# Residual sums bank by bank, a finer last gate and a reordered opening in a float32 encoder trunk

## What is computed

```python
h = x
for i in range(2):
    hn = rms_norm(h, norm_mix[i])
    if i == 0:
        h = h + concat(attention(hn @ w_in), conv(hn @ w_in)) @ w_out
        h = h + swiglu(rms_norm(h, norm_ffn[0]), wg, wu, wd)        # 1024 x 2816
    else:
        h = h + pool(hn) * pool_scale
        h = h + sum(gates[:, e] * swiglu(rms_norm(h, norm_ffn[1]), wg[e], wu[e], wd[e]) for e in range(8))
    gate = sigmoid(rms_norm(h, ple_norm[i]) @ ple_gate_w[i])        # 1024 x 1024
    h = h + gate * (p[i] @ ple_proj[i])                             # 256 x 1024
```

## Time and profile before

| | |
|---|---|
| median of 3 runs | 1361.47 us (1361.33 to 1363.37) |
| profiled execution | 1361.89 us |
| its span | 1360.1 us |
| TensorE busy | 1335.8 us, 98% |
| VectorE busy | 1156.1 us, 85% |
| ScalarE busy | 1008.5 us, 74% |
| granted TensorE clock | 0.999 |

### The profile page before, as it was taken

The page is one execution under the profiler, slowest core; times in us unless marked ns, Lnnn a source line. Parts: engine busy times, 40 slices in busy tenths (PEclk is TensorE's granted clock), DMA queues, the critical chain, the costliest instruction groups (busy, mean ns, idle before and its releaser), DMA issues.

```text
span 1360.1 us, 19059 instructions
## 1 busy us (share of the span) xinstructions
PE 1335.8 (98%) x6747; PEld 1126.5 (83%) x6747; DVE 1156.1 (85%) x1241; ACT 1008.5 (74%) x1188; POOL 46.9 (3%) x55
## 2 busy tenths in 40 slices
PE   7999999999999999999999999999999999999998
PEld 6868999988778888888888888888888888888886
DVE  6986555557799999999999999999999999999995
ACT  6866444446788887888888788888878888888874
POOL 1000000000050000000000000000000000000000
PEclk9999999999999999999999999999999999999999
DMA  9407853376799899999999999999999999999930
GB/s 350 163 1 272 301 186 124 125 250 235 110 379 397 309 394 395 374 360 396 394 339 394 395 374 359 396 395 339 394 395 374 359 396 394 394 393 398 400 122 33
DMA packets 178484, 427.03 MB, mean 314 GB/s; under 512 B 4096, under 2 KB 13568, under 8 KB 178432
## 3 DMA queue, kind: packets, MB, share of 16 engines
q1 hardware_dynamic: 173248, 412.10, 80.9%
q0 software_dynamic: 3168, 11.54, 3.3%
q10 hardware_dynamic: 2016, 2.72, 0.6%
HBM read 419.53 MB, written 6.82 MB: 313 GB/s over the span
## 4 chain that ended last, share of the span: by engine, by line
PE 91%; DVE 5%; ACT 2%; issue 1%; DMA 0%; SPq 0%; ACTq 0%; DVEq 0%
PE G L1366 18%; PE G L1368 18%; PE G L1367 18%; PE Y L1366 11%; PE Y L1368 11%; PE Y L1367 11%; PE G L1712 2%; DVE lo_ring L803 2%; DVE ring L863 1%; DMA ring<-in_w_in 0%; ACT xT_hi L504 0%; ACT tok L561 0%; DVE xT_lo L833 0%; ACT hi_ring L468 0%; DVE s_small L934 0%
## 5 line engine op out<-in xcount | busy, mean ns | idle before, releaser
L803 DVE TENSOR_TENSOR lo_ring<-ring,hi_ring 128x1024 fp32r<-128x1024 f32 x692 | 838.3, 1224 | 141.6 <-ACT hi_ring L468 100.1
L468 ACT ACTIVATE hi_ring<-ring 128x1024 fp32r<-128x1024 f32 x692 | 732.8, 1062 | 250.5 <-PE G L1368 149.0
L1366 PE MATMUL G<-hi_ring,xT_hi 128*128 128x512 f32 x896 | 353.9, 395 | 1.4 <-DVE lo_ring L803 0.8
L1368 PE MATMUL G<-lo_ring,xT_hi 128*128 128x512 f32 x896 | 349.5, 390 | 0.0
L1367 PE MATMUL G<-hi_ring,xT_lo 128*128 128x512 f32 x896 | 348.8, 389 | 0.0
L1366 PE MATMUL Y<-hi_ring,mT_hi 128*128 128x512 f32 x568 | 223.9, 394 | 0.0
L1368 PE MATMUL Y<-lo_ring,mT_hi 128*128 128x512 f32 x568 | 221.3, 390 | 0.0
L1367 PE MATMUL Y<-hi_ring,mT_lo 128*128 128x512 f32 x568 | 221.2, 389 | 0.0
L1366 PEld LDWEIGHTS G<-hi_ring,xT_hi 128*128 128x128 f32 x896 | 168.2, 188 | 36.0 <-DVE lo_ring L803 2.0
L1368 PEld LDWEIGHTS G<-lo_ring,xT_hi 128*128 128x128 f32 x896 | 168.3, 188 | 35.8
L1367 PEld LDWEIGHTS G<-hi_ring,xT_lo 128*128 128x128 f32 x896 | 168.4, 188 | 33.5
(11 more groups left out here) (251 smaller groups left out, 939.6 us busy)
## 6 DMA issues: line engine op xcount, KB each, us to landing
ring<-in_moe_wg SPq DMA_DIRECT2D x56, 2048.0 KB, 11.8
ring<-in_moe_wu SPq DMA_DIRECT2D x56, 2048.0 KB, 13.3
ring<-in_moe_wd SPq DMA_DIRECT2D x56, 2048.0 KB, 13.2
ring<-in_ffn_wg SPq DMA_DIRECT2D x5, 2048.0 KB, 11.5
ring<-in_ffn_wu SPq DMA_DIRECT2D x5, 2048.0 KB, 10.1
ring<-in_ffn_wd SPq DMA_DIRECT2D x5, 2048.0 KB, 7.9
ring<-in_ple_gate_w SPq DMA_DIRECT2D x4, 2048.0 KB, 7.8
ring<-in_w_out SPq DMA_DIRECT2D x2, 2048.0 KB, 13.4
```

What stands on the lines that cost most here:

```text
L468: act.activation(hi_ring[:, n % AHEAD, :], where, ACT.Copy).then_inc(hi_done, 1)
L803: dve.tensor_tensor(lo_ring[:, n % AHEAD, :], where, hi_ring[:, n % AHEAD, :].bitcast(F32), ALU.subtract).then_inc(lo_done, 1)
L1366: pe.matmul(dst, s_hi, m_hi, start=start, stop=False, skip_group_check=True)
L1368: return pe.matmul(dst, s_hi, m_lo, start=False, stop=stop, skip_group_check=True)
```

## The change

Five places are edited; what is computed stays the same.

1. Opening: TensorE transposes all eight blocks of token tile 0, then those of tile 1. ScalarE and VectorE make weight piece 0, four blocks, piece 1, four blocks.
2. Output projection: bank 2c + t takes the place of 2t + c, so that the left halves of both tiles are done first; the last two pieces go bank by bank. VectorE adds four times 512 columns; `half_ready` marks the left halves. The transposes of the left half wait for these, and those of the last two blocks for all. On ScalarE norm 1's copies go ahead of piece 25.
3. First gate: bank b's first product waits for the low copies of blocks 2b and 2b + 1.
4. Last expert and gate: the spread matmuls, the additions and the transposes go by column halves as in 2; the second projection piece is cut in two by token tiles, one behind each half of the transposes; the wait goes by banks as in 3; on VectorE the low copies go ahead of one low part; the last three pieces (two before) go bank by bank, behind one wait for their three low parts.
5. End: the last bank's sigmoid, product, addition and store are cut in two of 256 columns.

```diff
+HALVED = (1, 5)
+LAST_PARTS = ((0, 0, 512), (1, 0, 512), (2, 0, 512), (3, 0, 256), (3, 256, 512))
 # SP
-        for t, c0, c1, n in ((0, 0, D, 2), (1, 0, 512, 3), (1, 512, D, 4)):
+        for t, c0, c1, n in ((0, 0, D, 2), (1, 0, 512, 3), (1, 512, 768, 4), (1, 768, D, 5)):
 # ScalarE
         norm(0)
+        hi_upto(0)
+        act.wait_ge(vec_in, 16)
+        norm_hi(0, Y8, 0, KT // 2)
         hi_upto(1)
-        act.wait_ge(vec_in, 16)
-        norm_hi(0, Y8)
+        norm_hi(0, Y8, KT // 2, KT)
...
+        hi_upto(20 + AHEAD)
+        norm_hi(1, Y8)
         hi_upto(21 + AHEAD)
-        norm_hi(1, Y8)
         norm(1)
...
-        for b in range(2 * T):
+        for n, (b, c0, c1) in enumerate(LAST_PARTS):
...
-            act.activation(tok[:, b // 2, (b % 2) * 512:(b % 2 + 1) * 512], Y[:, b, :], ACT.Sigmoid,
+            act.activation(tok[:, b // 2, (b % 2) * 512 + c0:(b % 2) * 512 + c1], Y[:, b, c0:c1], ACT.Sigmoid,
 # VectorE
-        def add_rows(i, use, end):
+        def add_halves(i, use, end):
+            for c in range(2):
+                for t in range(T):
+                    b = 2 * c + t
+                    dve.wait_ge(bank_done, 3 * use + b + 1) if b < 3 else dve.wait_ge(pe_piece, end)
+                    dve.tensor_tensor(h[:, t, c * 512:(c + 1) * 512], h[:, t, c * 512:(c + 1) * 512], Y[:, b, :],
+                                      ALU.add).then_inc(h_ready if c else half_ready, 1)
...
+        lo_upto(0)
+        norm_lo(0, Y8, 0, KT // 2)
         lo_upto(1)
-        norm_lo(0, Y8)
+        norm_lo(0, Y8, KT // 2, KT)
...
-            for t in range(T):
-                dve.wait_ge(scat_mm, t + 1)
...
+            for c in range(2):
+                for t in range(T):
+                    part = h[:, t, c * 512:(c + 1) * 512]
+                    dve.wait_ge(scat_mm, 2 * c + t + 1)
...
+            norm_lo(5, Y8)
             last(XP + AHEAD)
-            norm_lo(5, Y8)
...
+        for n, (b, c0, c1) in enumerate(LAST_PARTS):
+            t, c = b // 2, slice((b % 2) * 512 + c0, (b % 2) * 512 + c1)
+            dve.wait_ge(sig_gate, 2 * T + n + 1)
+            link(dve.tensor_tensor(tok[:, t, c], tok[:, t, c], G[:, b, c0:c1], ALU.mult))
+            dve.tensor_tensor(h[:, t, c], h[:, t, c], tok[:, t, c], ALU.add).then_inc(gated, 1)
 # TensorE
+        def norm_half(i, bank, half):
...
+                for k in range(half * KT // 2, (half + 1) * KT // 2):
+                    if i in HALVED:
+                        if half == 0 and t == 0 and k % 2 == 0:
+                            pe.wait_ge(half_ready, T * HALVED.index(i) + k // 2 + 1)
+                        if half and t == 0 and k == KT - 2:
+                            pe.wait_ge(h_ready, T * (i + 1))
...
-        def rows(n, s_hi, s_lo, bank, first, last):
+        def rows(n, s_hi, s_lo, bank, first, last, freed=None):
...
+                    if freed is not None:
+                        pe.wait_ge(nlo_done, freed + 2 * (2 * t + c + 1))
...
+        def last_out_rows(n, e):
+            for u in range(2):
+                pe.wait_ge(lo_done, n + u + 1)
+            for c in range(2):
+                for t in range(T):
+                    for u in range(2):
+                        w_hi, w_lo = hi_ring[:, (n + u) % AHEAD, :], lo_ring[:, (n + u) % AHEAD, :]
+                        ins = three(Y[:, 2 * c + t, :], ...)
+                        if (c, t) == (1, T - 1):
+                            piece(n + u, ins)
+                    if (c, t) != (1, T - 1):
+                        ins.then_inc(bank_done, 1)
...
-        norm(0, Y8)
+        for t in range(T):
+            pe.wait_ge(tok_done, t + 1)
+            for k in range(KT):
+                ins = pe.transpose(Y8[:, k, t * P:(t + 1) * P], tok[:, t, k * P:(k + 1) * P], ident)
...
-            pe.wait_ge(nlo_done, KT * 3)
             for k in range(KT - 3):
-                rows(first + 2 + k, xT_hi[:, k, :], xT_lo[:, k, :], Y, k == 0, False)
+                rows(first + 2 + k, xT_hi[:, k, :], xT_lo[:, k, :], Y, k == 0, False, None if k else KT * 2)
...
-            norm(5, Y8)
-            last_rows_of(XP + 1, pT_hi[1][:, 1], pT_lo[1][:, 1], G, False, True)
-            pe.wait_ge(nlo_done, KT * 6)
+            for t in range(T):
+                norm_half(5, Y8, t)
+                last_rows_of(XP + 1, pT_hi[1][:, 1], pT_lo[1][:, 1], G, False, True, (t,))
...
+            for u in range(3):
+                pe.wait_ge(last_lo, XP + KT - 1 + u - AHEAD + 1)
+            for b in range(2 * T):
+                t, c = b // 2, slice((b % 2) * 512, (b % 2 + 1) * 512)
+                for u in range(3):
+                    q, k = XP + KT - 1 + u, KT - 3 + u
+                    ins = three(Y[:, b, :], ...)
```

More of the change, by code:

```diff
@@ L1044, in _ @@
         lo_upto(PB - 2)
-        gate(0)
+        gate()
         dve.wait_ge(gate_add, 2 * T)
@@ L1555, in _ @@
         ins.then_inc(mean_mm, 1)
-        rows(14, mT_hi[:, 0, :], mT_lo[:, 0, :], Y, True, False)
+        out_rows(14, 0, True)
         pe.wait_ge(sq_done, 1)
```

113 lines of the change are left out of this document (57 added, 56 removed).

## The result

The changed kernel takes 1356.01 us (median of 6 executions, 1355.69 to 1356.60) against 1361.42 (median of 6, 1361.10 to 1363.37): a ratio of 0.9955 on record, 95% interval 0.9944 to 0.9965 (the quotient of the two medians is 0.9960, inside it). The forecast was 1357.4, a fall of 4.1, in a range of 1356.0 to 1359.4; the fall is 5.4. The direction was right, the size was 1.4 us short, and the time lies on the lower edge of the range. The profiled execution takes 1355.81 us and its span is 1354.0; that of before took 1361.89, so the two profiles differ by 6.08.

A forecast was written before the change was run, and what follows sets the result against it. TensorE was taken to bound the kernel, with time to be had only where it stands still. 1.1 + 1.08 + 0 + 1.5 - 0.1 + 0.8 = 4.4 us off the profiled 1361.89 or median 1361.47 gave 1357.4, range 1356.0 to 1359.4.

The forecast's parts named there:

- Opening, 1.1: Before the first weight product: reordered transposes and copies start TensorE's products at 11.85, 1.1 us earlier (0 to 1.2).
- rival (a): Clock: the opening's first products run at half pace, losing 0.55 us, so 1357.9; chance 0.20.
- Output projection, 1.08: Residual after the output projection: banks by column half let copies start at 119.87, 1.08 us earlier (0.7 to 1.15).
- rival (b): Absorbed: ScalarE or VectorE takes up one of the two early gains, so 1358.5; chance 0.15.
- First gate, 0 (0 to 0.35): Dense half's first gate product: spread waits remove 0.34 us at 318.35, but TensorE waits longer at 333.82; no gain.
- Last expert, 1.5 (1.2 to 1.65): Residual before the last gate: idle falls from 1.8 to some 0.3 us, first gate product 1.5 earlier.
- The end, 0.8 (0.5 to 1.2): After the last matmul: last addition gains 0.6 us and the smaller store 0.2.
- passes stay: Sign in the seven expert passes: each stays at 119.04 us, or the prediction is wrong.
- no wait 36 matmuls from the end: Sign in the last gate: no wait before its last three pieces, for which 0.1 us (0 to 0.3) was charged.
- The wait at 333.82 longer: Sign behind the dense half's first gate: TensorE's wait for a low part there grows once the 0.34 at 318.35 goes.
- Rival (c): End edit fails: the three-piece wait costs 1.2 us, not 0.1, halves give 0.5, not 1.5; 1359.5; chance 0.10.
- rival (d): Slower: instructions come late at seven expert loop turns and the loop's end, 1.49 us each; 1369; chance 0.05.

The follow-up runs named there:

- e5: The changed kernel run and profiled again with no edit; 1357.05 us, ratio 0.9953 to the kernel before.
- e1: The kernel before run and profiled again with no edit; 1363.32 us median of 11, ratio 1.000.
- e13: The kernel before with nine transposes of a constant added ahead of the first real one; 1361.67 us, ratio 0.9995.
- e4: The kernel before with the six transfer issues (pooling scales and bands) moved from ScalarE's queue to GpSimd's; 1361.69 us, ratio 0.9996.
- e6: The changed kernel with the six transfer issues (pooling scales and bands) moved from ScalarE's queue to GpSimd's; 1356.13 us, ratio 0.9949.
- e2: The kernel before with only the first gate's waits by banks added; 1361.75 us median of 11, ratio 0.9994.
- e7: The changed kernel with the last bank of the final gate whole again and three stores for four; 1356.96 us, ratio 0.9956.
- e3: The changed kernel with the single wait for all low copies at the first gate put back; 1357.07 us median of 5, ratio 0.9956.
- e9: The changed kernel with the last gate's matmuls tile by tile over two pieces as before, last bank still split; 1357.56 us, ratio 0.9962.

## Why the prediction was right in direction and short in size

**Opening, 1.1:** right. The first product came at 11.91 (11.85 said), A moved by 1.04, and the shift at 50 was that at 13. The pitch behind it was 0.12 at once in the two first profiles, so rival (a) did not come in their times. Yet its mechanism is real: 4 to 7 products are slow in four of the other profiles with the new opening and 1 or 2 in two more (up to 0.8 us: the first 48 products take 5.83 in after and 6.61 in e5), and 22 in e1. What I had wrong is that I weighed it for the change alone. It burdens the kernel before more, by 2.1 us in half of its executions, and I had three times of that kernel before me, one of them 1363.37, and did not ask what set it apart.

**Output projection, 1.08:** right to the hundredth, with ScalarE's leeway of 0.28 where 0.3 was said. No rival (b).

**First gate, 0 (0 to 0.35):** this is the step that failed, 1.04 in the profiles and 0.9 to 1.06 in the medians. It failed twice. First, the claim that TensorE would only wait longer at 333.82, and so give the gain back, rested on one execution with a long transfer issue (1.47), which made ScalarE's chain late; e1 and e13 show the kernel before without that wait, and the chain has slack there. With the edit and short issues only 0.14 to 0.17 comes back at W2. Second, the bound of 0.35 took the idle time on the row as the price of the wait. The pair e4 and e6 prices it at 0.64: the idle is counted from the modelled end of the last matmul, 0.39 after its start, but without the wait the next one would start 0.23 after it, which adds 0.16, and the first matmul behind the wait is followed after 0.34, not 0.23, which adds 0.11. That makes 0.61. With W2's 0.20 of idle for 0.50, the two waits of the earlier trace rows were worth 1.15 and not 0.54. So of the 1.04 about half is the edit by itself (0.64 less the 0.16 at W2), which the bound of 0.35 also missed; the other half is the long issue's wait, which was in before's profile and not in after's. It goes in most executions and not in all (e2).

**Last expert, 1.5 (1.2 to 1.65):** the mechanism was right and the size off: 1.80 from C to D, with the 0.1 for three pieces already in it (0.05 to 0.1 measured), so about 1.9 for 1.5. Up to the gate's first product it is 1.72. I had left 0.3 of idle; 0.07 is left. And by the same error as above, three waits (0.50, 0.55 and 0.36 by their rows) cost more than their idle.

**The end, 0.8 (0.5 to 1.2):** 0.86, right in both terms, 0.60 and 0.26 for 0.6 and 0.2. The prediction had the reason too: "VectorE is free when the last bank comes" is the spacing, worth 0.64, and "without that split the last addition would end 0.1 earlier" is the cost of the short operations, 0.04. The second follows the rule of the Trainium skill that the prediction cites for it (VectorE: DVE Perf Modes, "The TRN2 errata"), and these rows agree with it. What was wrong is the text ahead of e7, which gives the split all of the 0.8: the split brings 0.21 (4.98 against 4.77), the store's 0.26 less the operations' 0.04.

**What was asked of the profile:** passes stay (118.99 against 119.04; e1 has 118.99 too and e5 119.04, so that this is the execution's time scale), no wait 36 matmuls from the end, last addition 2.59 after the last matmul, the wait at 318.35 gone: as said. The wait at 333.82 longer: not so in after, but so in e2. Rival (c) and rival (d) did not occur. The prediction's times for the rivals are right but for two: (b) with both gains taken up is 1357.4 + 2.18 = 1359.6 and not 1359.3, and (c) at 1359.5 lies just outside the range that it was to be in for the most part. The profiled execution of before was 0.47 above its median and that of after 0.20 under its own; that is why the profiles differ by 6.08 and the medians by 5.4.

In the sum: forecast 4.4, profiles 6.08; the difference of 1.7 is 1.0 for the first gate, 0.4 for the last expert, 0.26 for the time scale of the two executions (the seven passes), and 0.06 for the end, less 0.06 in the opening.

## What to carry to other kernels

Price a wait of TensorE by the matmuls' starts across it against the same run of matmuls without one, not by the idle time on its row: here 0.34 stood for 0.64 and 0.20 for 0.50. Before a gain is written off because another chain would be late next, see in a second execution whether that chain is late there too, above all when one row in it (a transfer issue of 1.47 among five of 0.45) is out of line. And when a queue of equal operations follows the last matmuls, space the banks by more than what one bank costs the next engine before cutting the last bank into smaller operations. Where a kernel's executions lie at two levels, find what parts them before a change to it is priced by medians.

## What was not expected of the hardware

- TensorE's pace can be halved for about 10 us of the start (7.9 to 17.8 in e1) while the granted clock reads 1.00. The moment of the rise changes from execution to execution: 12.8, 13.5, 13.6 and 13.7 in e3, e7, e9 and e5, 17.8 in e1, and ahead of the first product in before and after. It made two levels of the kernel before's time, 1361.5 and 1363.6.
- Of the six transfer issues on ScalarE's queue, those that started while an instruction transfer ran, or 0.07 ahead of it, lasted until 0.37 us after its end: 0.90 to 1.47 us in place of 0.45. Four more, near 133 us, took 1.43 to 1.63, and four near 365 us that met a transfer took 0.33 all the same. On SyncE's queue most issues beside such transfers stayed at 0.37.
- From B to C the kernels take 969.25 to 969.78 us (once 970.23), from one execution to the next and whatever the edit; the kernel before has both 969.25 and 969.56.
